# Merging the high and low activations of six MLP phases into one 512-column matmul

## What is computed

```python
u2 = rmsnorm_2(h, norm2_g[l])                                        # u2: 256 x 2048
h = h + jnp.square(jax.nn.relu(u2 @ mlp_w1[l])) @ mlp_w2[l]          # mlp_w1: 2048 x 8192, mlp_w2: 8192 x 2048
```

## Time and profile before

| | |
|---|---|
| median of the runs | 2661.3 us (2654.89 to 2662.23) |
| the profiled execution | 2656.17 us |
| its span, first to last instruction | 2654.4 us |
| mean granted TensorE clock | 0.998 of 2.4 GHz |
| TensorE matmuls | 23008, busy 2642.0 us (100%) |
| VectorE | busy 1668.1 us (63%) |
| ScalarE | busy 1280.7 us (48%) |
| DMA | 503.49 MB, 190 GB/s on the mean |
| the eight MLP phases | the last 696 us of matmuls |

### The profile page before, as it was taken

One profiled execution on the slowest core, in us unless ns is written; L12 is line 12 of the kernel. 1 busy time (PEld: TensorE's weight loads), 2 busy tenths in 40 slices (PEclk: granted clock), 3 DMA queues, 4 the chain that ended last, 5 costly groups with the idle time before them and its releaser, 6 DMA issues.

```text
span 2654.4 us, 54434 instructions
## 1 busy us (share of the span) xinstructions
PE 2642.0 (100%) x23008; PEld 2634.1 (99%) x23008; DVE 1668.1 (63%) x1755; ACT 1280.7 (48%) x1460; POOL 1.6 (0%) x13
## 2 busy tenths in 40 slices
PE   9999999999999999999999999999999999999999
PEld 8999999999999999999999999999999999999999
DVE  6664655566776576567675787676666555565554
ACT  6444444445554454455553466664444344343443
POOL 0000000000000000000000000000000000000000
PEclk9999999999999999999999999999999999999999
DMA  7556666666666666666666666666666666666664
GB/s 215 157 161 193 195 192 194 193 194 196 190 195 191 197 193 195 192 196 191 193 184 179 176 187 192 193 191 192 196 192 193 197 191 194 195 193 196 192 194 139
DMA packets 265387, 503.49 MB, mean 190 GB/s; under 512 B 17703, under 2 KB 26591, under 8 KB 265183
## 3 DMA queue, kind: packets, MB, share of 16 engines
q1 hardware_dynamic: 262916, 500.53, 64.4%
q10 hardware_dynamic: 2282, 0.26, 0.1%
HBM read 498.63 MB, written 2.10 MB: 189 GB/s over the span
## 4 chain that ended last, share of the span: by engine, by line
PE 98%; DVE 1%; DMA 1%; ACT 0%; issue 0%; SPq 0%; ACTq 0%; DVEq 0%
PE psum L573 30%; PE psum L572 30%; PE psum L574 30%; PE psum L599 2%; PE psum L601 2%; PE psum L600 2%; DMA raw<-in_w_in 1%; DVE wlo L1361 0%; PE psum L827 0%; PE psum L828 0%; PE psum L826 0%; ACT whi L909 0%; PE psum L696 0%; DVE hn L1421 0%; PE psum L888 0%
## 5 line engine op out<-in xcount | busy, mean ns | idle before, releaser
L1361 DVE TENSOR_TENSOR wlo<-raw,whi 128x1024 fp32r<-128x1024 f32 (+1 forms) x952 | 1149.6, 1215 | 748.0 <-ACT whi L909 746.2
L909 ACT ACTIVATE whi<-raw 128x1024 fp32r<-128x1024 f32 (+1 forms) x952 | 991.4, 1052 | 1051.7 <-DMA raw<-in_mlp_w 351.5
L573 PE MATMUL psum<-hn,whi 128*128 128x256 f32 x4448 | 1230.7, 277 | 0.0
L574 PE MATMUL psum<-hn,wlo 128*128 128x256 f32 x4448 | 1230.0, 277 | 0.0
L572 PE MATMUL psum<-hn,whi 128*128 128x256 f32 x4435 | 1228.2, 277 | 1.4 <-DVE hn L1421 1.2
L572 PEld LDWEIGHTS psum<-hn,whi 128*128 128x128 f32 x4435 | 834.0, 188 | 4.0 <-issue 2.1
L574 PEld LDWEIGHTS psum<-hn,wlo 128*128 128x128 f32 x4448 | 836.9, 188 | 0.0
L573 PEld LDWEIGHTS psum<-hn,whi 128*128 128x128 f32 x4448 | 836.5, 188 | 0.0
L573 PE MATMUL psum<-act,whi 128*128 128x256 f32 x2544 | 702.4, 276 | 0.0
L574 PE MATMUL psum<-act,wlo 128*128 128x256 f32 x2544 | 702.2, 276 | 0.0
L572 PE MATMUL psum<-act,whi 128*128 128x256 f32 x2540 | 701.1, 276 | 0.0
(11 more groups left out here) (253 smaller groups left out, 972.3 us busy)
## 6 DMA issues: line engine op xcount, KB each, us to landing
raw<-in_w_in SPq DMA_DIRECT2D x320, 512.0 KB, 3.7
raw<-in_mlp_w SPq DMA_DIRECT2D x256, 512.0 KB, 3.8
raw<-in_w_up SPq DMA_DIRECT2D x160, 512.0 KB, 4.3
raw<-in_w_down SPq DMA_DIRECT2D x84, 512.0 KB, 4.1
raw<-in_w_out SPq DMA_DIRECT2D x64, 512.0 KB, 3.8
raw<-in_w_branch_m SPq DMA_DIRECT2D x16, 512.0 KB, 3.7
raw<-in_w_branch_c SPq DMA_DIRECT2D x16, 512.0 KB, 3.7
raw<-in_w_up SPq DMA_DIRECT2D x16, 384.0 KB, 3.3
```

Of the source, the lines that this page charges most:

```text
L573: mm(o, hi[:, kk, w], both[:, 1, :], start=False, stop=False)
L574: last = mm(o, lo[:, kk, w], both[:, 0, :], start=False, stop=end and (m % 2 == 1 or m == tiles - 1))
L909: A(filled(whi[:, n % SLOTS, :], ph, i, loc), filled(raw[:, n % SLOTS, :], ph, i, loc), ACT.Copy)\
L1361: V.tensor_tensor(filled(wlo[:, n % SLOTS, :], ph, i, loc), filled(raw[:, n % SLOTS, :], ph, i, loc), filled(whi[:, n % SLOTS, :].bitcast( ...
```

## The change

Six of the eight MLP phases, all but the first and the last, are put in a tuple DOUBLE. In them a tile's high weights meet high and low activations in a single matmul of 512 columns, which fills a whole bank; the low weights still meet the high activations, in the first 256 columns of the bank. The two halves of the bank are summed afterwards: ScalarE copies the second half of all four banks into `low_half` (a part of `misc` that is free by then), and VectorE adds first and second half, into `ysum` in mlp1 and in two additions into `h` in mlp2. In mlp1 the multiplication by the scale then becomes an operation of its own. In the first group of a double mlp2 phase the first 512-column matmul of the last half is issued as two of 256. The core of the diff:

```diff
+DOUBLE = ("mlp2_0", "mlp1_1", "mlp2_1", "mlp1_2", "mlp2_2", "mlp1_3")
...
+        low_half = view(misc, 0, GW, T)
...
+                        if ph.name in DOUBLE:
+                            for m in range(GW):
+                                o = psum[:, 4 * s + m, :].rearrange("p (a t) -> p a t", t=T)
+                                w = slice(m * P, (m + 1) * P)
+                                if k == halved and kk == 0 and m == 0:
+                                    mm(o[:, 0, :], hi[:, kk, w], both[:, 0, :], start=False, stop=False)
+                                    mm(o[:, 1, :], hi[:, kk, w], both[:, 1, :], start=False, stop=False)
+                                else:
+                                    mm(o, hi[:, kk, w], both, start=first, stop=False)
+                                last = mm(o[:, 0, :], lo[:, kk, w], both[:, 0, :], start=False, stop=end)
+                            continue
...
-                            at = 1 if each else MIDDLE + 1 if m else int(2 * ph.chunks) - 1 if w and name[:4] == "down" else halved if first and s == 1 else None
+                            at = 1 if each else MIDDLE + 1 if m else int(2 * ph.chunks) - 1 if w and (name[:4] == "down" or name in DOUBLE) else halved if first and s == 1 else None
...
+            def copy_low(ph, i, s):
+
+                ac.wait_ge(half_used, 1 + 2 * ph.c0 + HB(ph) * i + (s + 1) * (HB(ph) // 2))
+                ac.wait_ge(psum_freed, ph.g0 + 2 * i + s + 2)
+                A(low_half, psum[:, 4 * s:4 * s + 4, T:2 * T], ACT.Copy).then_inc(sem("low_copied"), 1)
...
+                    if j == 0 and ph.name in DOUBLE:
+                        copy_low(ph, i, s)
...
+            def into_residual(j, ph, i, s):
+                if j == 0:
+                    copy_low(ph, i, s)
...
-                left = run(f"mlp2_{q}", residual(20) if q == 3 else nothing, left)
+                left = run(f"mlp2_{q}", residual(20) if q == 3 else into_residual, left)
...
+            def low_ready(ph, i, s):
+
+                ve.wait_ge(sem("low_copied"), GW * DOUBLE.index(ph.name) + 2 * i + s + 1)
+                ve.wait_ge(half_used, 1 + 2 * ph.c0 + HB(ph) * i + (s + 1) * (HB(ph) // 2))
+                return psum[:, 4 * s:4 * s + 4, 0:T]
+
+            def add_both(j, ph, i, s):
+
+                if j == 0:
+                    t = h[:, ds(GW * (2 * i + s), GW), :]
+                    link(V.tensor_tensor(t, t, low_ready(ph, i, s), ALU.add))
+                    V.tensor_tensor(t, t, low_half, ALU.add).then_inc(psum_freed, 1)
...
-                        scaled_total(ph, i, s, ysum)
-                        totalled(ph, i, s)
+                        if ph.name in DOUBLE:
+                            o = low_ready(ph, i, s)
+                            V.tensor_tensor(ysum, o, low_half, ALU.add).then_inc(psum_freed, 1)
+                            totalled(ph, i, s)
+                            link(V.tensor_tensor(ysum, ysum, over_tiles(stream_scale), ALU.mult))
+                        else:
+                            scaled_total(ph, i, s, ysum)
+                            totalled(ph, i, s)
```

More of the change, by code:

```diff
@@ L2035, in _ @@
                            first=(lambda x: scale_from_root(5) if x == MIDDLE + 1 else None) if q == 0 else None)
-                left = run(f"mlp2_{q}", residual(*((20, None, None, False, True) if q == 3 else ())), left)
+                left = run(f"mlp2_{q}", residual(20, None, None, False, True) if q == 3 else add_both, left)
             left = finish(left)
```

## The result

The changed kernel takes 2681.84 us (median of four runs, 2678.53 to 2683.56) against 2658.1 us before (four runs, 2652.93 to 2662.23): a ratio of 1.0092, 95% interval 1.0077 to 1.0106. It is slower by 0.9%, some 24 us, where no difference was forecast and the range ended at 2670. The spans of the two profiled executions are 24.0 us apart too (2678.4 against 2654.4). The runs of one kernel fall into two groups, 4 to 8 us apart, and of either kernel two lie in each, so the medians can be compared.

The account below looks back on a forecast made before the run. The pace of TensorE's matmuls was taken to bound the kernel. 1533 x (226.7 + 113.3 - 340.0) = 0 on TensorE and 0 for the rest, laid on the median, gave 2661.3 us, range 2645 to 2670.

Parts of the forecast that it names:

- X: Start-to-start time of a 512-column matmul in the six double MLP phases, put at 226.7 ns, twice that of 256 columns.
- the triple: Three 256-column matmuls per tile in the MLP phases, 340.0 ns; as one of 512 and one of 256, forecast unchanged.
- The sum of the prediction: Over the double phases, 1533 x (226.7 + 113.3 - 340.0) = 0 us on TensorE, and 0 for the rest.
- The rule for the surcharge: Time TensorE matmuls take beyond their columns: 8 clocks for each 128 columns begun, so 544 clocks for 512 columns.
- (a): TensorE in double phases: surcharge of 16 clocks per instruction, 512 columns take 220.0 ns, 10.2 us saved, 2651.1 us; chance 0.20.
- (b): TensorE in double phases: long matmuls run at the array's rate, 215 ns, 17.9 us saved, 2643.4 us; chance 0.16.
- (c): Double phases: surcharge grows past 256 columns, 512 take 232.1 ns, 8.3 us more, 2669.6 us; chance 0.13 with (d).
- the late copy: ScalarE's added copy out of PSUM makes activations late for mlp2 starts; chance 0.13 together with (c).
- The cover: Added ScalarE and VectorE work in double phases lies beside the matmuls and costs nothing, with margins of 5 us or more.
- (d): At four mlp2 starts ScalarE's copy delays activations; beyond 5 us slip, each us costs 1 us per start; 0.13 with (c).

## Why the prediction was wrong, and where it held

**The step that failed** is the one from "X = 226.7 ns, exactly twice 113.3" to "the triple stays at 340.0 ns": it took for granted that a matmul's pace follows from its shape alone, and that a matmul changes nothing for the ones behind it. X was worked out as 226.7 ns, and the 256-column matmul behind it was left at 113.3. The first 512-column matmul took 226 ns, in the changed kernel and in each of the others that had one. In the changed kernel all later ones took 235.0, and their partners 118.3: 13.3 ns a pair more than forecast. The sum of the prediction with these is 1533 x 13.3 = 20.4 us, plus 3.4 us for mlp2_3, which it had named as a phase that must keep its 87.0: 23.8, with 24.0 measured. So the size was right for the first 512-column matmul and wrong for all behind it; the cause, one such matmul being enough, is shown by the runs with one extra matmul.

**The evidence was in the trace.** The 117 and 114 ns of the earlier trace rows belong to the same two shapes a microsecond or two apart, and I averaged them to 115.5 instead of asking why they differ. The cut matmuls of the earlier trace rows were read for what they cost and not for what they do to the pace. A look at line 573 by stretches would have shown 281 ns against 276. The base had the same thing in it: the 5.1 us between the profiled execution and the median of three runs, which I laid on the median, is about what a stretch at the slow pace from 172 to 338 us costs in the executions above. For runs without a profile that is not shown, but with a fourth run the median fell to 2658.1.

**The rule for the surcharge** was half right. "8 clocks for each 128 columns begun" was fitted to 123.3 ns at 272 columns, but that holds in a row of such matmuls; alone in a quick stretch 272 columns take 120 ns. 17/16 of a clock a column fits 256, 272, 384 and the first 512. That merging saves nothing is upheld in each state: 768 columns take 340.0 ns as three matmuls in one and 353.3 ns as two or as three in the other. Rivals (a) and (b), a surcharge of the instruction (220.0) and X = 215, are refuted by the same 226 ns. The Trainium skill, page "TensorE: Matmul & The Clock Gate", section "Back-to-back issue gap", states N/2.4 + 2.5 ns for a warm matmul, which makes 215.8 ns the estimate for 512 columns. Neither pace here agrees: 226 and 235 ns were measured, with fp32r operands.

**Rival (c)** had the sign, and 232.1 of the 235.0 ns, with 2669.6 us. Its mechanism (a surcharge that grows with the length) is not what happened, since the 256-column matmuls were slowed as well, and so its price came to 8.3 of the 24 us: it left these at 113.3 ns and did not reach into mlp2_3. A chance of 0.13 for it and the late copy was too low for a shape that no row showed. (The chances by direction, 0.37, 0.48 and 0.15, should be 0.38, 0.47 and 0.15 by the prediction's own split.)

**The cover held.** ScalarE's copy out of PSUM took 1.03 us (1.2 assumed). Behind the end of mlp1_1, at 2214.1, after the change:

```profile
2215.43 1.23 DVE L2063 TENSOR_TENSOR work<-psum,misc 128x1024 f32<-128x1024 f32 x1 [3.53 <-ACT misc L929]
2216.69 1.23 DVE L2065 TENSOR_TENSOR work<-work,scale 128x1024 f32<-128x1024 f32 x1
2217.95 1.23 DVE L2070 SCALAR_TENSOR_TENSOR work<-work 128x1024 f32<-128x1024 f32 x1
...
2222.39 1.22 DVE L1409 TENSOR_TENSOR act<-work,act 128x1024 fp32r<-128x1024 f32 x1
```

The low part is done at 2223.6, 9.5 us after the phase's start (10.9 assumed, 7.3 by the earlier trace rows), and is wanted at 17 us. No matmul waited, and the run with the merging undone prices all of it at nothing. Rival (d), a wait in the place of the gain, didn't happen (it would have struck at three starts of mlp2 and not four, since mlp1_0 isn't double). Over the kernel VectorE is busy for 26.1 us more and ScalarE for 21.1, where 29 each were forecast.

**What stays open** is what the state is. It isn't the level of the granted clock, which is 1.00 in both. It doesn't need a long matmul: the float32 sums in mlp1_0 bring it about too. The experiments show three things that start it (one matmul of 512 columns, a row of 272, the float32 sums) and one that ends it, a matmul of 256 columns issued as two of 128: in the twelve traces the quick pace follows each of the 76 such cuts behind 150 us that meet the slow pace among matmuls of 256. The list isn't complete. The drop of the clock near 170 us is in ten of the twelve traces; TensorE comes out of it at the quick pace in seven, among them the changed kernel, which had gone into it at the slow one, and at the slow pace in three. In the first 112 us of the kernel before, the slow pace ends three times without a cut (at 29.7, 87.3 and 111.1 us), and one cut, at 74.4 us and right behind a rise of the clock, doesn't end it. I have no rule that tells beforehand which length does what, nor whether the moment matters. No version here beats the kernel before; the one with the merging undone equals it.

## What to carry to other kernels

Before counting on fewer and longer matmuls, read the pace of those there are from start to start: if it follows the columns (here 17/16 of a clock each for fp32r), merging has nothing to win. Read it by stretches too, in every phase, since the same instruction may run at two paces at one clock. Where a kernel holds an odd instruction that costs time and computes nothing new, such as one matmul cut in two, look for what the pace does ahead of it and behind it. A change in a phase that TensorE bounds is then to be judged in the phases behind it too, and where one of them has slowed down untouched, that is the place to look.

## What the hardware showed that I had not expected

- TensorE ran back-to-back fp32r matmuls of 256 columns at 113.3 or at 117.8 ns, both at a granted clock of 1.00, and kept to either for long: some 710 us at 117.8 in the kernel without its cut. The duration in the profile tells them apart, 276 against 281 ns.
- One matmul of 512 columns (226 ns) moved it from the first to the second for the rest of the kernel; one of 384 (170 ns) or 256 did not; one of 272 (120 ns) did for under a microsecond.
- The same kernel code can come out of a 3 us drop of the granted clock to 0.50 at either pace; between 175 and 339 us that made 6 us of difference.
- Splitting one 256-column matmul into two of 128 moved it back, worth 3.4 us for each phase of 768 matmuls that follows; where the pace was quick already, such a cut costs some 0.11 us.
